# Memory keys and values of both layers projected inside the even attention, in whole groups between twos of units

## The reference

```python
def memory_xattn(h, m, wq, wkv, qg, kg, wo):
    q = rmsnorm((h @ wq).reshape(bsz, seq, M_HEADS, M_DIM), qg)
    k, v = jnp.split(m @ wkv, 2, axis=-1)
    k = rmsnorm(k.reshape(bsz, -1, M_HEADS, M_DIM), kg)
    v = v.reshape(bsz, -1, M_HEADS, M_DIM)
    logits = jnp.einsum('bshd,bmhd->bhsm', q, k) * M_DIM ** -0.5
    p = jax.nn.softmax(logits, axis=-1)
    o = jnp.einsum('bhsm,bmhd->bshd', p, v).reshape(bsz, seq, M_HEADS * M_DIM)
    return o @ wo
# called with rmsnorm(h, mem_norm) and rmsnorm(mem, src_norm); M_HEADS = 4, M_DIM = 128
```

## Time and profile before

| | us |
|---|---|
| three runs | 1787.21, 1781.81, 1754.67 |
| median | 1781.81 |
| profiled execution, device time | 1782.73 |
| its span in the trace | 1780.7 |
| even projection to the end of even attention's norms | 759 to 923.7 in the trace |
| even output projection | 923.7 to 947.5 |
| memory part of layer 0: queries; keys and values; attention; output | 947.5 to 960.5; to 987.9; to 998.4; to 1012.8 |
| memory part of layer 1: the same | 1523.0 to 1536.5; to 1563.9; to 1574.4; to 1589 |

### The profile page before, as it was taken

How to read it: one execution, slowest core, us unless ns; L and a number is a source line. 1 busy time by engine, 2 the same in 40 slices (tenths; PEclk the granted TensorE clock), 3 DMA queues, 4 the chain that set the end, 5 groups by cost and what they waited for, 6 DMA issues and landing times.

```text
span 1780.7 us, 25000 instructions
## 1 busy us (share of the span) xinstructions
PE 1685.5 (95%) x10388; PEld 1508.9 (85%) x10388; DVE 1070.8 (60%) x1557; ACT 848.5 (48%) x1217; POOL 14.4 (1%) x22
## 2 busy tenths in 40 slices
PE   7969899889998999999789999999999999999999
PEld 7857788789987999888567899989998887789997
DVE  4554546578865555476766665546564766665553
ACT  4444344366645444354345644435443555664442
POOL 0000000000000000000000000000000000000000
PEclk9965699999999999999589999999999999999999
DMA  7723045455453554455014455545455441435553
GB/s 277 272 100 125 1 162 196 156 183 174 183 191 147 183 190 188 167 193 185 24 48 166 143 198 181 188 168 194 182 190 189 180 174 64 162 107 189 187 183 127
DMA packets 42976, 290.21 MB, mean 163 GB/s; under 512 B 5048, under 2 KB 5198, under 8 KB 9968
## 3 DMA queue, kind: packets, MB, share of 16 engines
q1 hardware_dynamic: 38272, 271.93, 42.1%
q0 software_dynamic: 4592, 16.69, 2.7%
HBM read 287.51 MB, written 8.55 MB: 166 GB/s over the span
## 4 chain that ended last, share of the span: by engine, by line
PE 89%; DVE 6%; DMA 2%; ACT 2%; issue 1%; DVEq 1%; SPq 0%; POOL 0%; ACTq 0%; POOLq 0%; PEldq 0%
PE bank L444 25%; PE bank L446 25%; PE bank L445 25%; PE bank L450 9%; DMA raw<-stream_dram 2%; PE bank L709 2%; PE bank L1382 2%; DVE low L412 1%; PE bank L596 1%; ACT high L401 1%; DVEq L2070 1%; PE bank L457 0%; DVE u L955 0%; DVE h L1076 0%; DVE u L649 0%
## 5 line engine op out<-in xcount | busy, mean ns | idle before, releaser
L401 ACT ACTIVATE high<-raw 128x2048 fp32r<-128x2048 f32 x257 | 489.2, 1915 | 558.1 <-DMA raw<-stream_dram 554.7
L412 DVE TENSOR_TENSOR low<-raw,high 128x2048 fp32r<-128x2048 f32 x255 | 581.7, 2289 | 247.9 <-ACT high L401 246.7
L444 PE MATMUL bank<-xh,high 128*128 128x256 f32 x1880 | 534.3, 284 | 1.1 <-DVE low L412 1.1
L445 PE MATMUL bank<-xl,high 128*128 128x256 f32 x1880 | 533.1, 284 | 0.0
L446 PE MATMUL bank<-xh,low 128*128 128x256 f32 x1880 | 532.9, 283 | 0.0
L444 PEld LDWEIGHTS bank<-xh,high 128*128 128x128 f32 x1880 | 362.1, 193 | 2.1 <-issue 1.4
L445 PEld LDWEIGHTS bank<-xl,high 128*128 128x128 f32 x1880 | 362.2, 193 | 0.0
L446 PEld LDWEIGHTS bank<-xh,low 128*128 128x128 f32 x1880 | 362.0, 193 | 0.0
L444 PE MATMUL bank<-high,xh 128*128 128x512 f32 (+2 forms) x528 | 204.7, 388 | 2.5 <-DVE low L412 1.6
L446 PE MATMUL bank<-high,xl 128*128 128x512 f32 (+2 forms) x528 | 202.8, 384 | 0.0
L445 PE MATMUL bank<-low,xh 128*128 128x512 f32 (+2 forms) x528 | 202.8, 384 | 0.0
(11 more groups left out here) (207 smaller groups left out, 1589.7 us busy)
## 6 DMA issues: line engine op xcount, KB each, us to landing
raw<-stream_dram SPq DMA_DIRECT2D x257, 1024.0 KB, 4.8
band_wide_dram<-band_rows_dram POOLq DMA_DIRECT2D x1, 3072.0 KB, 22.5
t_wide_dram<-t_rows_dram POOLq DMA_DIRECT2D x1, 2304.0 KB, 15.4
u<-mem_dram POOLq DMA_DIRECT2D x2, 1024.0 KB, 5.2
bias<-band_wide_dram POOLq DMA_DIRECT2D x1, 2048.0 KB, 14.9
rel_wide_dram<-rel_rows_dram POOLq DMA_DIRECT2D x1, 1920.0 KB, 16.3
bias<-t_wide_dram POOLq DMA_DIRECT2D x1, 1536.0 KB, 7.9
bias<-rel_wide_dram POOLq DMA_DIRECT2D x1, 1280.0 KB, 7.5
```

The costliest lines, as they stand in the source:

```text
L401: act.activation(self.high[:, n % RING, :], self.raw[:, n % RING, :], ACT.Copy).then_inc(self.high_split, 1)
L412: dve.tensor_tensor(self.low[:, n % RING, :], self.raw[:, n % RING, :], self.high[:, n % RING, :].bitcast(F32), ALU.subtract).then_inc(sel ...
L444: pe.matmul(out, lh, rh, start=start, stop=False)
L445: pe.matmul(out, lh, rl, start=False, stop=False)
```

## The change

The keys and values of both layers are projected inside the even attention, and the two stages that projected them are gone.

- Stream order: `wkv0` and `wkv1` (4 slots each) stand between `even` and `even_out`. Their splits multiply by the gain of the source norm (`gained_pieces`), four pieces of 512 a slot.
- `MemoryProject` is `Project` with a load of the memory rows by POOL behind it: once in the small projection of the first block (into `c.o`), whose next stage `Rope` makes the rows' norms with ACT and DVE, and once in the even projection (into `c.u`, after the first three batches are turned).
- `Select` turns the memory rows behind its scores of block 0: 4 x 4 transposes, 4 copies, 4 subtractions of 128 x 512.
- The even attention is now `Paired` with `Fill`. PE issues, for a two of units: turns, scores (the two units' matmuls alternate), values of the two before, and then one whole group of 24 matmuls. There are 8 groups: 2 layers, 2 halves (keys, values), 2 blocks. ACT drains a group with the row's norm as scale. Outputs of a two share a bank, and DVE waits for both.
- `Residual` of both output projections norms and turns the memory keys: PE behind tiles 0 to 3, ACT and DVE ahead of the later splits.
- The query stage now norms and turns its queries itself, behind its only job.

```diff
@@ stream_plan
-            plan += [("even_tail", KT, S), ("even", 7 * KT, HALF), ("even_out", 2 * KT, HALF)]
+            plan += [("even_tail", KT, S), ("even", 7 * KT, HALF), ("wkv0", 2 * KT, HALF), ("wkv1", 2 * KT, HALF),
+                     ("even_out", 2 * KT, HALF)]
...
-        plan += [(f"wq{layer}", KT, HALF), (f"wkv{layer}", 2 * KT, HALF), (f"wo{layer}", 8, HALF)]
+        plan += [(f"wq{layer}", KT, HALF), (f"wo{layer}", 8, HALF)]
@@ split_low (split_high likewise)
+            if n in self.gained:
+                for cut, gain in self.gained_pieces(n):
+                    last = dve.scalar_tensor_tensor(self.low[:, n % RING, cut], self.raw[:, n % RING, cut], gain,
+                                                    self.high[:, n % RING, cut].bitcast(F32), ALU.mult, ALU.subtract)
@@ Residual.tensor, behind tiles 0 to 3
+        if self.turn:
+            self.input_wait(pe, s, KT - 1)
+            self.turn.turn_rows(pe, s, 0)
@@ Residual.scalar
+        if self.turn:
+            self.turn.square_rows(act, s, 0)
+            c.split_high(act, self.m.first)
+            self.turn.copy_high(act, s, 0)
         c.split_high(act, self.m.slot(self.m.count - 1))
@@ Residual.vector
+        if self.turn:
+            self.turn.scale_rows(dve, s, 0, Steps(dve, s["dve_step"]))
+            c.split_low(dve, self.m.first)
+            self.turn.copy_low(dve, s, 0)
         c.split_low(dve, last + 1 - LEAD)
@@ Fill
+    def tensor(self, pe, s, g):
...
+        if g:
+            pe.wait_ge(s["fill_stored"], g)
+        for k in range(KT):
...
+            w = c.piece(pe, m, i0 + k)
+            last = mm3(pe, c.bank[self.BANK][:, :], (xh[:, k, block_cut(b)], xl[:, k, block_cut(b)]), w,
+                       k == 0, k == KT - 1)
@@ Paired.tensor
+        def score(i):
+            if i >= 4:
+                pe.wait_ge(s["logits_ready"], i - 2)
+            for j in range(2):
+                for n, u in enumerate(units[i:i + 2]):
+                    if j < u.n:
+                        last = mm(pe, self.scores(i + n)[:, j, :], u.q[j], u.k[j], True, True)
...
+        score(0)
+        score(2)
+        self.groups.tensor(pe, s, 0)
+        for i in range(0, len(units) + 2, 2):
+            if i < len(units):
+                turn(i)
+                turn(i + 1)
+            if i + 4 < len(units):
+                score(i + 4)
+            if i:
+                value(i - 2)
+                value(i - 1)
+            self.groups.tensor(pe, s, i // 2 + 1)
@@ Paired.scalar
+        for i in range(0, len(units), 2):
+            if i + 2 < len(units):
+                exp(i + 2)
+                exp(i + 3)
+            copy(i)
+            copy(i + 1)
+            self.groups.split_high(act, i // 2 + 1)
+            self.groups.store(act, s, i // 2 + 1)
@@ Paired.vector
+        for i in range(0, len(units) + 2, 2):
+            if i + 2 < len(units):
+                logits(i + 2)
+                logits(i + 3)
+            if self.select and i < 8:
+                self.select.search(dve, step, 4 + i // 2)
+            if i:
+                finish(i - 2)
+                finish(i - 1)
+            self.groups.split_low(dve, i // 2 + 1)
@@ Rope
+        dve.wait_ge(s["norm_squares"], NB)
+        dve.tensor_scalar(c.inv[:, 6:8], c.inv[:, 6:8], 1.0 / D, EPS, ALU.mult, ALU.add).then_inc(s["norm_means"], 1)
+        dve.wait_ge(s["norm_roots"], 1)
+        dve.reciprocal(c.inv[:, 6:8], c.inv[:, 6:8])
@@ memory_stages
-    out = [Project(c, x, [(wq, 0, range(KT), HALF, [u[:, b, D:D + HALF] for b in range(NB)])],
-                   source=Source(c, c.h, x, gain=f"l{layer}_mem", norm=True), scale=True),
-           Project(c, x, [(wkv, n * KT, range(KT), HALF, [u[:, b, n * HALF:(n + 1) * HALF] for b in range(NB)])
-                          for n in range(2)], source=Source(c, mem, x, gain=f"l{layer}_src", norm=True), scale=True,
-                   batches=[both, None])]
+    queries = head_batch(c, 2 * D, HALF, 4, f"mq{layer}", P)
+    out = [Project(c, x, [(wq, 0, range(KT), HALF, [u[:, b, 2 * D:2 * D + HALF] for b in range(NB)])],
+                   source=Source(c, c.h, x, gain=f"l{layer}_mem", norm=True), scale=True, batches=[queries])]
@@ stages_of (odd_out likewise)
-            st.append(Residual(c, "even_out", turned, KT, loads=Loads((c.u[:, :, 2048:3072], mem))))
+            st.append(Residual(c, "even_out", turned, KT, turn=memory_keys(c, 0)))
```

More of the change, by code:

```diff
@@ L326, in __init__ @@
         self.unsplit = range(phi.first, phi.first + phi.slots)
+        self.gained = {}
+        for layer in range(2):
+            m, n = self.plan[f"wkv{layer}"], ROWS.index(f"l{layer}_src") * KT
+            for i in range(0, m.count, m.per):
+                self.gained[m.slot(i)] = n + i % KT
         self.top = -(-nc.sbuf_base // 64) * 64
@@ L400, in split_high, with gained_pieces @@
             act.wait_ge(self.slot_loaded[n % RING], 16 * (n // RING + 1))
-            act.activation(self.high[:, n % RING, :], self.raw[:, n % RING, :], ACT.Copy).then_inc(self.high_split, 1)
+            if n in self.gained:
+                for cut, gain in self.gained_pieces(n):
+                    last = act.activation(self.high[:, n % RING, cut], self.raw[:, n % RING, cut], ACT.Copy, scale=gain)
+                last.then_inc(self.high_split, 1)
+            else:
+                act.activation(self.high[:, n % RING, :], self.raw[:, n % RING, :], ACT.Copy).then_inc(self.high_split, 1)
             self.act_next = n + 1
+    def gained_pieces(self, n):
+        for j in range(SLOT // HALF):
+            k = self.gained[n] + j
+            yield slice(j * HALF, (j + 1) * HALF), PARAM(self.param, "gains")[:, k:k + 1]
     def split_low(self, dve, last):
@@ L1475, in vector, with __init__, first_blocks, last_slot @@
                 finish(i - 2)
+class Fill:
+    BANK = 5
+    def __init__(self, core, groups, x):
+        self.core, self.groups, self.x = core, groups, x
+    def first_blocks(self, g):
+        return sum(b < NB - 1 for _, _, b, _, _ in self.groups[:g + 1])
+    def last_slot(self, g):
+        m, i0, b, place, factor = self.groups[g]
+        return m.slot(i0 + KT - 1)
+    def arrive(self, pe, s, g, k):
+        pass
+    def tensor(self, pe, s, g):
+        if g >= len(self.groups):
+            return
+        c = self.core
+        m, i0, b, place, factor = self.groups[g]
+        xh, xl = self.x
+        if g:
+            pe.wait_ge(s["fill_stored"], g)
+        for k in range(KT):
+            self.arrive(pe, s, g, k)
+            w = c.piece(pe, m, i0 + k)
+            last = mm3(pe, c.bank[self.BANK][:, :], (xh[:, k, block_cut(b)], xl[:, k, block_cut(b)]), w,
+                       k == 0, k == KT - 1)
+            if b == NB - 1:
+                c.release(last, m, i0 + k)
+        if b < NB - 1:
+            last.then_inc(s["fill_summed"], 1)
+    def split_high(self, act, g):
+        if g < len(self.groups):
+            self.core.split_high(act, self.last_slot(g) + self.groups[g][2] - NB + 1)
+    def split_low(self, dve, g):
+        if g < len(self.groups):
+            self.core.split_low(dve, self.last_slot(g) + self.groups[g][2] - NB + 1)
+    def store(self, act, s, g):
+        if g >= len(self.groups):
+            return
+        c = self.core
+        m, i0, b, place, factor = self.groups[g]
+        if b == NB - 1:
+            act.wait_ge(c.slot_used, self.last_slot(g) + 1)
+        else:
+            act.wait_ge(s["fill_summed"], self.first_blocks(g))
+        act.activation(place, c.bank[self.BANK][:, :], ACT.Copy, scale=factor).then_inc(s["fill_stored"], 1)
@@ L1750, in vector @@
             dve.wait_ge(s["out_taken"], i + 1)
-            if b == 1:
+            if b == 0:
+                self.memory.vector(dve, s, i)
+            else:
                 self.search(dve, step, i % 4)
```

190 lines of the change are left out of this document (170 added, 20 removed).

## The result

The changed kernel took 1796.12 us, the median of four executions (1792.42 to 1798.75), against 1780.18 for the kernel before, the median of four executions beside it. The ratio is 1.011, 95% interval 1.006 to 1.016. So it is some 16 us slower by the medians. The profiled execution took 1796.62 us with a span of 1794.8, against 1780.7 before.

The account below looks back on a forecast made before the run. PE, busy 95% of the span, was taken as the bound. Removed stages (-54.9 us) against added terms, the paired attention's +24.9 largest, gave +1.5 on 1780.7: span 1782.2, forecast 1784 us, range 1753 to 1796.

Parts of the forecast that it names:

- the lead is used up and not overdrawn; the cover is about 2 us: Paired even attention: DVE starts two twos ahead, so PE stays the bound; otherwise it ends up to 3 us later.
- the forecast's own sign of being wrong: Even attention over 80 us, PE gaps inside it ended by DVE, or a clock staying down; 71 to 78 us expected.
- Rival 4: Paired attention: DVE becomes the bound, or scores go one after the other; +5 to +10, about 1792 us; chance 0.11.
- The terms of PE in that stage: Paired attention: turns 6.1, values 11.0, scores 7.0, groups 43.6, changes 1.2, clock 2.8, end 1.2; 72.9 us against 48.0.
- the opening row: Odd attention's six opening score matmuls, past in 1.06 us, taken as showing that both partition halves run at once.
- rival 3: Paired attention: the clock never recovers; +65 us, about 1849; chance 0.04.
- Select: 16 memory-row transposes at half clock, 3.67 us, one us falling into waits; block 1's scores 2.7 us later (bounds 1 and 4).
- The front: Before the even attention: memory-row norms in Rope +0.8 us; POOL's two memory loads cost nothing, 1 to 4 if late.
- Output projections: Both output projections: key turns 0.9 and a 3.3 us PE stall at the fourth slot each, +8.4; clock +2.4.
- even odds: Output projections: the roughly 3.3 us gap may let the clock fall; 1.2 us each, +2.4 (0 to 5).
- Query stages and memory attention: Query norms and turns uncovered, +6.3 us per layer, +12.6; memory attentions begin at 1.2 GHz, +4.6 (bounds 0 and 10).
- Rival 2: First attention's 63 us half-clock stretch runs at full clock, not aimed at by the change; 1756 us; chance 0.20.

Follow-up runs that it names:

- the split moved: Changed kernel with ACT's high split of the next slot issued ahead of its turn's exponentials and copies in the paired attention: 1789.52 us median.
- the run with idle matmuls: Kernel before, with 24 idle matmuls issued first in the even attention only: 1782.12 us, ratio unclear around 1.00 (0.988 to 1.014).
- its first six variants above: Changed kernel with one edit each: high split first 1789.52, fewer group matmuls 1792.16, fourth slot earlier 1788.19, memory load earlier 1796.46, query gap filled 1789.24, turns moved 1792.74 us.

## Why the prediction was wrong

The forecast was 1784 us with a range to 1796; it came to 1796.12. That the change is slower and within 2% was right; the sum was 12.6 us short (1794.8 of span against 1782.2), and two thirds of that are one step.

**The failed step: "the lead is used up and not overdrawn; the cover is about 2 us".** The forecast compared each engine's work per turn with PE's: DVE 9.5 in its dearest turns, ACT 6.4, PE 7.9 to 9.0. As loads these were about right: with the split moved, DVE works almost without a pause and its turns are 8.9 to 9.1 us, later 7.3 to 7.4, where 9.5 and 7.4 to 7.6 were forecast. It added up loads and never followed an item through the two engines. Low split waits for high split, high split stood behind the exponentials in ACT's list, these wait for logits, and the logits stand behind the low split in DVE's list. A turn is therefore the length of that round trip, 9.2 to 9.9 us, though neither engine is ever full. PE's lead lasts to 915; from there the stage goes at the ring's pace. Price: 81.2 against 72.9, +8.3 us, of which some 1.7 are the last value products at a clock that the ring's gaps had let fall; over 80 us was the forecast's own sign of being wrong. The run with one line moved took it away (72.3), and the run with a third of PE's instructions removed did not. Rival 4 (DVE the bound, 1792) had the nearest time, but not the mechanism: DVE's work is unchanged in the kernel that takes 72.3. A rival missing from the list decided: a wait between ACT and DVE that neither's load shows.

**The terms of PE in that stage held.** Scores of two units of block 1 took 1.07 us to the next start for four matmuls on alternating halves, where two on one half take 1.05; the opening row had said so. This trace agrees with the rule that the Trainium skill states in "TensorE: Matmul & The Clock Gate" (Part 3, packing small matmuls).

```profile
890.61 1.14 PE L477 MATMUL bank<-t 64*128 64x256 f32 x8
891.68 0.49 PE L477 MATMUL bank<-u,prob_t 128*128 128x128 f32 x2
```

The clock was back at 1.00 4 us into the stage, where 4.3 was forecast, so rival 3 did not occur; the later fall at 936 is the ring's doing and was gone with the split moved. The reading of the earlier trace rows, that much of the even attention's 48 us was the same work at 1.2 GHz, was right for some 6 us; beyond that the run with idle matmuls shows DVE busy almost without a pause. The sum did not need this reading, because it was built from full-clock rows.

**Select: +5.0 for +2.7.** The price of 16 transposes at half clock was right: 3.8 us on the chain for 3.67. But "one us falls into waits" was not. PE goes from score to transposes without a pause, and that its four scores of block 0 themselves follow each other at half clock (4.1 us, where before block 0 was past in 2.85 with its waits) was priced at nothing. 2.4 us came back when the transposes were moved.

**The front: +3.5 for +0.8.** "The two memory loads are issued by POOL, whose queue holds nothing else there; I cost it at nothing." The meeting of that stage waits for POOL, and POOL 5.3 us behind its load; `Rope` began 1.6 us late. The norms of the memory rows added 0.5 (PE waits 4.71 us from its last transposes to the first product of `Compress`, against 4.22), and 1.2 of the remaining 1.4 us is in `Compress`, where the clock rose at another moment in the two traces. That last part is not shown to come from the change.

**Output projections: 10.3 for 10.8.** Gaps of 3.08 and 3.19 us for 3.3. The clock fell in one of the two, at 1544, as even odds had it.

**Query stages and memory attention: +12.5 and +4.4 for +12.6 and +4.6.** The chain read from the earlier trace rows and the half clock behind the gap came as forecast, and filling the gap took the second away.

**Rival 2** did not occur in the four executions, but the short form is real. The spread of the runs is this: of 66 executions of before, 17 were under 1760 us, and the trace of a short execution of before with the filled even attention shows the first attention in 60 us where the traced long one took 90. In the changed kernel and its first six variants above (31 executions) only two stand apart, 1768 and 1772, each over 20 us under the median of its variant; they have no trace, but they look like the short form. The change may have made it rarer; that was not tested.

## What to carry to other kernels

Adding up each engine's work per turn bounds a loop from below only. Where two engines hand to each other twice in one turn (a split in two parts, and a softmax in two parts), walk one item through both lists and add up the round trip; if it exceeds the largest load, reorder so that what the other engine waits for stands first. And a stage whose PE is shown busy for 92% can be one that PE doesn't bound: here a third of its work could go and the turns stayed the same to 0.01 us. Last, when two versions of a stage come out equally long, compare them piece by piece before calling the edit without effect: 6.1 us won and 6.2 lost look like nothing.

## What the hardware showed that was not expected

- The clock's fall in an attention whose PE is shown busy without a pause decides 30 us of one kernel: the same 350 PE instructions took 89.6 us (mean clock 0.58, busy 83.55) or 60.2 (0.90, busy 54.61).
- Idle matmuls against it are not a matter of more: 3 behind each unit left it to chance, 2 held it in sixteen executions of sixteen. The paired attention, with whole groups of 5.45 us among the units, stayed at 1.00 for as long as PE had no gap; in after the clock fell behind one of 2.05 us, and with the split moved it stayed up to the end.
- POOL's end of stage took 5.29 us behind a load of 1 MB that it had just issued and that nobody needed yet.
